# ScalarE's order in two attentions: a head pair's copies ahead of the next pair's exponentials

## The reference, cut to what matters

```python
logits = einsum("qhd,qkhd->qhk", q_b, k) * scale
logits = where(visible, logits, -inf)      # a query block sees the keys up to its own block
p = softmax(logits, axis=-1)
o = einsum("qhk,qkhd->qhd", p, v)
```

## Time and profile before

| | us |
|---|---|
| median of 3 runs (lowest to highest) | 3208.28 (3207.35 to 3209.14) |
| the profiled execution, its time | 3210.21 |
| the profiled execution, its span | 3208.4 |

### The profile page before, as it was taken

How to read it: one execution, slowest core, us unless ns; L and a number is a source line. 1 busy time by engine, 2 the same in 40 slices (tenths; PEclk the granted TensorE clock), 3 DMA queues, 4 the chain that set the end, 5 groups by cost and what they waited for, 6 DMA issues and landing times.

```text
span 3208.4 us, 40231 instructions
## 1 busy us (share of the span) xinstructions
PE 3088.7 (96%) x15372; PEld 2027.0 (63%) x15516; DVE 1676.8 (52%) x3462; ACT 944.3 (29%) x1464; POOL 1502.0 (47%) x788
## 2 busy tenths in 40 slices
PE   8999998898999999997998999999999999999998
PEld 6888785687677877885776444666655444444444
DVE  6433698548754341007424998444441255556664
ACT  2001225424641011115122223333333322222222
POOL 4664469755035664565556333333333333333331
PEclk9998999999999999998999999999999999999999
DMA  3222122123323222221223344444444656655551
GB/s 142 105 83 105 55 103 54 40 82 114 128 103 114 96 99 105 92 105 47 79 105 132 131 157 157 168 187 196 193 179 190 226 206 209 209 207 200 196 195 65
DMA packets 139832, 429.99 MB, mean 134 GB/s; under 512 B 8640, under 2 KB 79424, under 8 KB 116544
## 3 DMA queue, kind: packets, MB, share of 16 engines
q1 hardware_dynamic: 125216, 353.40, 30.9%
q10 hardware_dynamic: 7200, 68.68, 5.1%
q0 software_dynamic: 7296, 6.31, 0.8%
HBM read 358.10 MB, written 73.40 MB: 134 GB/s over the span
## 4 chain that ended last, share of the span: by engine, by line
PE 83%; DVE 11%; ACT 3%; issue 2%; DMA 1%; POOL 0%; SPq 0%; ACTq 0%; DVEq 0%; POOLq 0%
PE bank L1084 14%; PE bank L1085 14%; PE bank L1086 14%; PE bank L1107 4%; PE bank L653 4%; PE bank L648 4%; PE bank L649 4%; PE bank L676 3%; PE bank L681 3%; PE bank L677 3%; PE bank L907 3%; PE bank L902 3%; PE bank L903 3%; ACT work L1383 1%; DVE hF L1728 1%
## 5 line engine op out<-in xcount | busy, mean ns | idle before, releaser
L2398 POOL TENSOR_TENSOR work<-ring,work 128x4096 bf16<-128x4096 f32 x64 | 531.1, 8298 | 905.0 <-ACT work L1529 905.0
L1085 PE MATMUL bank<-work 128*128 128x512 bf16 x2004 | 761.2, 380 | 11.3 <-POOL work L2398 9.1
L1084 PE MATMUL bank<-work 128*128 128x512 bf16 x2005 | 761.7, 380 | 5.8 <-DVE work L2236 2.8
L1086 PE MATMUL bank<-work 128*128 128x512 bf16 x1991 | 756.1, 380 | 2.3
L2422 POOL CAST w_parts<-ring 128x1024 fp32r<-128x1024 f32 (+3 forms) x212 | 233.2, 1100 | 657.5 <-DMA ring<-in_wstream 156.7
L2424 POOL TENSOR_TENSOR w_parts<-ring,w_parts 128x1024 fp32r<-128x1024 f32 (+3 forms) x212 | 515.7, 2433 | 17.0
L2236 DVE TENSOR_TENSOR work<-hF,work 128x512 bf16<-128x512 f32 x128 | 307.7, 2404 | 253.0 <-ACT work L1613 249.9
L1084 PEld LDWEIGHTS bank<-work 128*128 128x128 bf16 x2048 | 200.8, 98 | 246.9 <-issue 14.0
L1086 PEld LDWEIGHTS bank<-work 128*128 128x128 bf16 x2048 | 200.8, 98 | 242.9 <-issue 2.2
L1085 PEld LDWEIGHTS bank<-work 128*128 128x128 bf16 x2048 | 200.7, 98 | 235.5 <-issue 1.7
L1529 ACT ACTIVATE work<-ring 128x4096 bf16<-128x4096 f32 x64 | 231.5, 3617 | 207.4 <-PE bank L1086 179.8
(11 more groups left out here) (341 smaller groups left out, 4967.9 us busy)
## 6 DMA issues: line engine op xcount, KB each, us to landing
ring<-in_wstream SPq DMA_DIRECT2D x128, 2048.0 KB, 7.7
hidden<-hF ACTq DMA_DIRECT2D x32, 1024.0 KB, 3.9
gates<-work ACTq DMA_DIRECT2D x16, 2048.0 KB, 8.3
hF<-hidden SPq DMA_DIRECT2D x32, 1024.0 KB, 6.7
work<-gates SPq DMA_DIRECT2D x32, 1024.0 KB, 10.1
rpb_tiles<-in_rpb POOLq DMA_DIRECT2D x192, 16.0 KB, 2.5
work<-rpb_tiles POOLq DMA_DIRECT2D x24, 128.0 KB, 4.1
ring<-in_wstream SPq DMA_DIRECT2D x5, 512.0 KB, 3.9
```

Of the source, the lines that this page charges most:

```text
L1084: pe.matmul(out, a(0), b(0), start=(start and k == 0), stop=False)
L1085: pe.matmul(out, a(0), b(1), start=False, stop=False)
L1086: mm = pe.matmul(out, a(1), b(0), start=False, stop=(stop and k == n - 1))
L2398: nc.gpsimd.tensor_tensor(SPLIT[:, p, 1, :], ring[:, p, :], SPLIT[:, p, 0, :], ALU.subtract).then_inc(lo, 1)
```

## The change

In ScalarE's `attention`, the two copies of step s stand ahead of the two exponentials of step s+1; before, they stood behind them. Nothing else differs: the same instructions with the same waits and signals, and the other engines' programs are as they were.

```diff
@@ -1395,12 +1395,12 @@
                 for s in range(-3, a.steps):
+                    if s >= 0:
+                        move(2 * s)
+                        move(2 * s + 1)
                     if -1 <= s < a.steps - 1:
                         exps(2 * s + 2)
                         exps(2 * s + 3)
-                    if s >= 0:
-                        move(2 * s)
-                        move(2 * s + 1)
                     for w in a.units_at(s):
                         move_qk(w)
```

## The result

The changed kernel takes 3229.31 us in the median of 4 runs (3225.95 to 3234.98), before 3207.82 (3206.37 to 3209.14): ratio 1.0066, 95% interval 1.0052 to 1.008. It is slower by 21.5 us; forecast were 15.0 (3223.3 us), range 3216 to 3234. The profiled execution took 3228.18 us with a span of 3226.4, 18.0 more than before.

The account below looks back on a forecast made before the run. It took "b" to be bound by a loop between VectorE and ScalarE, "c" by TensorE's queue. "b" 6.0 plus "c" 9.0 gave 15.0 us, so 3223.3 us; own range 3218 to 3231, eight in ten 3216 to 3234.

Parts of the forecast that it names:

- "b", blocks 0 and 3: Attention b: exponentials wait behind scaling, transposes and copies; +0.71 us at block 0, +0.10 at block 3, seven times each.
- Blocks 1 and 2: Attention b: no charge, because VectorE does 0.68 us of other work first and the copies are short.
- the first unit and the end: Attention b: +0.86 us in the first unit, partly at 1.2 GHz; -0.5 us at the end from earlier copies.
- the term taken as 0 within 3.2: Last unit of b: GpSimd's splitting slows scalings beside it; change taken as 0, bounded by -3.2 to +3.2 us.
- "c", block 3: Attention c: copies delay exponentials, then the copy of q and k and the scores; +1.10 us per passage, seven times.
- Block 0: Attention c: second exponential +1.26 us later, covered by TensorE's load in six units, counted once in the last.
- the rival by the clock: Both attentions: an emptier TensorE drops to a lower clock, adding +3.5, +3 and +3, to 3233 us; chance 0.13.
- A sign that the prediction named as against it: The forecast called itself wrong if, among other signs, the clock fell inside the steady units.
- a longer end of "b": Last unit of b: upper room of +3.2 us in the range, for GpSimd's splitting beside the scalings.
- block 2: Attention b: some 0.2 us a unit if VectorE's lateness didn't cover it; 1.4 us kept for the range.
- block 0 of "c" in every unit: Attention c: if the +1.26 us counted in every unit, 7.6 us more, an upper bound used in part.
- the last transposes of "b": End of b: the last four transposes, 0.97 us, start at about 605.67 and end at 606.64 in place of 607.23.

Follow-up runs that it names:

- the run with it alone: Kernel of before, with the copies put first only ahead of query block 0's exponentials, in both attentions; ratio 1.0041 (1.0023 to 1.006).
- an undisturbed run of the same order: Changed kernel, with GpSimd's split of weights for c's projection held until c's last output is taken; ratio 1.0092 (1.0057 to 1.0126).
- "b" alone: Kernel of before, with the copies put first in attention b only, c keeping the old order; ratio 1.0033 (1.0015 to 1.005).
- the late split on the order of before: Kernel of before, with GpSimd's split of weights for c's projection held until c's last output is taken; ratio 1.0062 (1.0031 to 1.0093).

## Why the prediction was right

**The mechanism and the sign** were right: ready exponentials wait behind scaling, transposes and copies. Units of 12.9 and 17.2 were forecast, 12.95 and 17.10 measured, at a full clock.

**"b", blocks 0 and 3.** The terms held one by one, with all copies first. From the exponential of block 2 to that of block 3 it was 3.06 us (572.14 to 575.20) and is 3.20 (565.70, ahead of the rows shown, to 568.90): +0.14 for +0.10. From block 3 to block 0 it was 2.97 (575.20 to 566.11 and a unit of 12.06) and is 3.71 (568.90 to 572.61): +0.74 for +0.71. Blocks 1 and 2 cost nothing, as said, while the others are late; alone they cost 0.1. They hold for this order alone: with the other copies left behind, blocks 0 and 3 cost 0.9 to 1.0 and 0.6.

**"b", the first unit and the end.** The first was 1.36 longer, 0.86 + 0.71 forecast. The last two together were 0.9 shorter than before, where 0.4 longer was forecast. That is where the term taken as 0 within 3.2, GpSimd's split, belongs; by these profiles it was about -1.3. But the two profiles of the kernel before differ by 1.2 in the same two units (32.0 and 30.9), so its size isn't shown. "b" gave +4.6 for 6.0.

**"c", block 3**: +1.10 a passage forecast; four undisturbed units (841.69 to 910.09 after, 829.28 to 893.33 before) grew by 4.35, 1.09 each. **Block 0** hidden, as the run with it alone shows.

**"c", the term that was missing** is GpSimd's contention: 2.1 us. The prediction has such a term for "b" alone and puts "c" at nothing without a word on it; there the unit beside the split was as long as the others. One low stretch in the second unit adds about 1.2 (16.87 against 15.67 in an undisturbed run of the same order). The rest of the difference between 11.8 and 9.0 is about -0.5: without its low stretch the second unit grew by 0.6 (15.67 against 15.03) for a forecast of 1.10. The first and the last unit grew by 3.3 and -0.8, together 2.5 for 2.4; a unit is cut at an exponential that comes later itself. That block 0 counts once, +1.26, fits the run with it alone: "c" grew by 3.8, 2.5 beside the split and 1.3 elsewhere.

**Between profile and median.** The median is 3.5 us further from before than the profile. The second profile of the changed kernel has "b" and "c" at +4.0 and +15.3, with two low stretches in "c". So the rival by the clock, with its chance of 0.13, holds in part: low stretches of 3.4 to 6.8 us cost 1 to 3 us each, by its own price of some 3 us for 7 us. A sign that the prediction named as against it, a clock that falls inside the units, was there in the second unit of "c". In all six profiles in which both copies went ahead of block 3 or of blocks 1 and 2 in "c" there were one to three of them there; of the eight others, one had any. That they come because TensorE waits longer fits, but no run here changed TensorE's load alone, so it stays argued.

**Luck.** The 15.0 were 6.5 short of 21.5. The room above 15.0 in the range was kept for a longer end of "b", for block 2 and for block 0 of "c" in every unit; none of these came. What used it was contention in "c" and low stretches, neither of which was in the range's sum (the clock stood beside it as a rival), while "b" came out 1.4 below its own. The units were foreseen; that the total fell inside is partly luck. Two steps of the working don't follow from its rows and change little: the bounds add up to 3219 and not 3218 at the low end, and the last transposes of "b" would start at 605.56, not 605.67.

## What to carry over

In an in-order queue an operation with an early input shouldn't stand behind one with a late input. Ask which of the two inputs was made last, and by whom. Here the copy needs the very last result of the engine that the exponential feeds. A wait of 0.1 to 0.7 us in a loop between two engines is paid in every turn. And when a change uses up the slack of the bounding engine, look for what that slack was hiding elsewhere: a contention whose unit isn't longer today may still be there, and a new timing can make it meet other instructions.

## What the runs showed of the hardware

The kernel of before and its variants have a second level of totals, some 16 us higher ("b" alone: eight executions from 3211 to 3219 us, four from 3231 to 3234). Two profiles show where it can come from, "b" alone and the late split on the order of before: TensorE ran at 1.2 GHz for some 31 to 34 us between 350 and 385 us, where the profile of before has a full clock. The stretch 345 to 390 us, first before, then "b" alone:

```profile
345.00:390.00 45.00, 43.58 (x171) 31.55 (x172) 40.05 (x99) 14.90 (x30) 13.81 (x8) 1.00 0.13 48
```

```profile
345.00:390.00 45.00, 43.03 (x113) 25.14 (x112) 24.23 (x54) 15.58 (x31) 4.15 (x3) 0.66 0.00 1
```

The same program up to there, 171 and 113 matmuls in the same time, and "b" begins at 520.4 in place of 502.4. Both edits act only later, so they have no part in it, and it fits that totals of one kernel lie in two groups; no profile of the kernel of before itself caught it. What sets it off is open. A second point: ScalarE's copies became a little longer where they wait for their transposes, by 15 to 18 ns in the mean of each shape (597 against 579 ns for 512 columns, 277 against 259 for 128).
